# A decoder step on one core: neighbouring cache rows go to one partition, and keys are put in order when they are turned

## The reference, cut to what matters

```python
def gather_attention(q, k_all, v_all, idx, dist, table):
    kg, vg = k_all[:, safe], v_all[:, safe]
    logits = jnp.einsum('bthgd,btmhd->bhgtm', q, kg) * ATTN_SCALE + bias
    logits = jnp.where(valid, logits, NEG_INF)
    ...
    o = jnp.einsum('bhgtm,btmhd->bthgd', p, vg)

def dilated_sample(q, k_all, v_all, L, table):
    for w, r in ((128, 1), (512, 4), (2048, 16)):
        idx = L + t - r * jnp.arange(w // r + 1)[None, :]    # t = 0..7
        ...
    return combine_branches(outs, lses)
```

## Time and profile before

| | |
|---|---|
| median of 3 runs | 1210.07 us |
| profiled execution, its own time | 1210.34 us |
| its span | 1208.6 us |
| granted TensorE clock, mean | 0.937 |
| PE busy | 1070.4 us (89%) |
| DVE busy | 588.0 us (49%) |
| ACT busy | 470.0 us (39%) |
| POOL busy | 137.8 us (11%) |
| hardware DMA queue | 96764 packets, 179.89 MB |

### The profile page before, as it was taken

How to read it: one execution, slowest core, us unless ns; L and a number is a source line. 1 busy time by engine, 2 the same in 40 slices (tenths; PEclk the granted TensorE clock), 3 DMA queues, 4 the chain that set the end, 5 groups by cost and what they waited for, 6 DMA issues and landing times. The chain is left out here.

```text
span 1208.6 us, 16319 instructions
## 1 busy us (share of the span) xinstructions
PE 1070.4 (89%) x5923; PEld 869.0 (72%) x5924; DVE 588.0 (49%) x972; ACT 470.0 (39%) x736; POOL 137.8 (11%) x133
## 2 busy tenths in 40 slices
PE   5799999999699998878999539999999999999960
PEld 3699999998456566645888437877877778778740
DVE  5411113420056664334335466664599966649534
ACT  5311111001256653234213224554377655546324
POOL 0000000000100000000000011312234422224120
PEclk8699999999779999998999759999999999999985
DMA  6125111201560006886322563678699966789338
GB/s 219 63 52 203 49 53 53 70 14 66 153 159 1 2 1 176 266 228 189 145 105 79 189 247 94 208 273 278 215 382 391 377 209 204 271 293 395 110 70 312
DMA packets 104161, 207.34 MB, mean 172 GB/s; under 512 B 12648, under 2 KB 47249, under 8 KB 104075
## 3 DMA queue, kind: packets, MB, share of 16 engines
q1 hardware_dynamic: 96764, 179.89, 41.7%
q0 software_dynamic: 7344, 26.74, 9.1%
HBM read 175.75 MB, written 36.55 MB: 176 GB/s over the span
## 5 line engine op out<-in xcount | busy, mean ns | idle before, releaser
L540 PE MATMUL bank<-xT_hi,w_hi 128*128 128x384 f32 (+1 forms) x432 | 96.3, 331 | 5.4 <-DVE w_rest L403 5.4
L540 PE MATMUL bank<-xT_rest,w_hi 128*128 128x384 f32 (+1 forms) x432 | 96.0, 330 | 0.0
L540 PE MATMUL bank<-xT_hi,w_rest 128*128 128x384 f32 (+1 forms) x432 | 95.7, 329 | 0.0
L1853 POOL DMA_INDIRECT x_rows<-y_out,out_id x24 | 58.5, 2437 | 216.0 <-DVE rows L1908 199.1
L994 DVE CUSTOM_DVE_ANT_0 logit<-score,stage 128x256 f32<-128x256 f32 (+7 forms) x80 | 46.1, 614 | 75.9 <-DMA sink_pick<-in_sink_pick 55.5
L1737 DVE TENSOR_TENSOR down_rest<-w_down,down_hi 128x2048 fp32r<-128x2048 f32 x32 | 71.9, 2289 | 20.9 <-ACT down_hi L1732 20.0
L540 PEld LDWEIGHTS bank<-xT_hi,w_hi 128*128 128x128 f32 x432 | 74.5, 190 | 5.6 <-issue 5.6
L1961 PE MATMUL gate<-gate_hi,rowsT_hi 128*128 128x512 f32 x192 | 77.2, 402 | 0.7 <-ACT rowsT_hi L1867 0.7
L1962 PE MATMUL gate<-gate_rest,rowsT_hi 128*128 128x512 f32 x192 | 77.7, 404 | 0.0
L1995 PE MATMUL y<-down_hi,hidT_hi 128*128 128x512 f32 x192 | 76.9, 401 | 0.0
L1962 PE MATMUL up<-up_rest,rowsT_hi 128*128 128x512 f32 x192 | 75.6, 394 | 0.0
(11 more groups left out here) (277 smaller groups left out, 2034.2 us busy)
## 6 DMA issues: line engine op xcount, KB each, us to landing
w_gate<-in_w_gate SPq DMA_DIRECT2D x16, 2048.0 KB, 12.1
w_up<-in_w_up SPq DMA_DIRECT2D x16, 2048.0 KB, 12.3
w_down<-in_w_down SPq DMA_DIRECT2D x16, 2048.0 KB, 12.7
stage<-in_w_in SPq DMA_DIRECT2D x6, 1536.0 KB, 7.1
k_cache<-in_cache_b_k SPq DMA_DIRECT2D x8, 768.0 KB, 7.9
bias_scratch<-bias_one_row SPq DMA_DIRECT2D x1, 5800.0 KB
mixT<-in_x_prompt SPq DMA_DIRECT2D x8, 512.0 KB, 4.0
x<-in_x_prompt SPq DMA_DIRECT2D x8, 512.0 KB, 4.0
```

What stands on the lines that cost most here:

```text
L540: ins = nc.tensor.matmul(bank[3 * (n % 2) + i][:, 0:m], w_tiles(wt, n // CH)[:, k, cols], xt[:, k, c:c + m], start=(k == 0 and x == 0), st ...
L1853: nc.gpsimd.indirect_dma_start(out=io["x1"], out_offset=bass.IndirectOffsetOnAxis(ap=out_id[:, :], axis=0), in_=y_out[:, :], in_offset=Non ...
```

## The change

Two or four neighbouring cache rows go to one partition: of the far rows partition p holds two neighbours (4 pairs of each 8), of the near rows four. Block k of the buffers then holds every second row (k = 0, 1) or every fourth (k = 2 to 5). Each buffer's far part is one DMA instead of two. The keys return to their order when the transposed block is copied: `key_cols(k)` gives the columns of `kT_s` that a block goes to, with a step of 2 or 4. Scores, bias and softmax stay as they are. The transposes of the probabilities pick the same columns with the same step, so that their rows match the V buffers. The semaphore counts follow the number of DMAs.

```diff
-                out, src = kT_s[:, b % 2, :, P * k:P * k + P], src[:, 0:BW].rearrange("p (g c) -> p g c", c=P)
+                out, src = kT_s[:, b % 2, :, key_cols(k)], src[:, 0:BW].rearrange("p (g c) -> p g c", c=P)
...
+        def key_cols(k):
+
+            return slice(k, FARK, 2) if k < 2 else slice(FARK + k - 2, FARK + NEARK, 4)
...
-                for k in range(2):
-                    sp.dma_start(k_cache[:, b % 2, k, :], io["cache_b_k_far"][b][k]).then_inc(k_loaded[b % 2], 16)
+                sp.dma_start(k_cache[:, b % 2, 0:2, :], io["cache_b_k_far"][b]).then_inc(k_loaded[b % 2], 16)
...
-                for k in range(2):
-                    sp.dma_start(to[:, k, :], io["cache_b_v_far"][b][k]).then_inc(loaded, 16)
+                sp.dma_start(to[:, 0:2, :], io["cache_b_v_far"][b]).then_inc(loaded, 16)
...
-                    pe.wait_ge(k_loaded[b % 2], 48 * (r + 1))
+                    pe.wait_ge(k_loaded[b % 2], 32 * (r + 1))
...
-                        ins = nc.tensor.transpose(bank[0:m, P * (x - k):P * (x - k) + P], probs[:, r % 2, P * x:P * x + m], ident[:, :])
+                        cols = key_cols(x) if x < SKT else slice(FARK + NEARK, SK)
+                        ins = nc.tensor.transpose(bank[0:m, P * (x - k):P * (x - k) + P], probs[:, r % 2, cols], ident[:, :])
...
-                    pe.wait_ge(v_place(b)[1], 64 if r == PAIRS - 1 else 64 * (r + 1))
+                    pe.wait_ge(v_place(b)[1], 48 if r == PAIRS - 1 else 48 * (r + 1))
...
-        io[f"cache_b_{n}_far"] = [[rows[b, 256 * k:256 * k + 256].rearrange("(a r) c -> a r c", r=16)[:, 0:NT, :]
-                                   for k in range(2)] for b in range(NB)]
-        io[f"cache_b_{n}_near"] = [rows[b, SEQ // 2:SEQ].rearrange("(k p) c -> p k c", p=P) for b in range(NB)]
+        io[f"cache_b_{n}_far"] = [rows[b, 0:SEQ // 2].rearrange("(a r k) c -> a r k c", r=8, k=2)[:, 0:NT // 2, :, :] for b in range(NB)]
+        io[f"cache_b_{n}_near"] = [rows[b, SEQ // 2:SEQ].rearrange("(p k) c -> p k c", p=P) for b in range(NB)]
```

## The result

The changed kernel takes 1213.64 us, median of 10 runs (1212.23 to 1215.58), against 1209.62 us of the kernel before in the same series (1208.55 to 1210.62). The ratio is 1.0029, 95% interval 1.0016 to 1.0041: 2 to 5 us slower. The prediction was 1214.5 us with a range of 1209.2 to 1219.5. The profiled execution took 1212.32 us (span 1210.6), 2.0 us more than that of the kernel before; the median lies 1.3 us above it.

What follows compares the result with a forecast made beforehand. The prediction took PE's chain with copies in it as the bound. Key pieces 3.4 us plus transposes of the probabilities 1.0 made 4.4 us; 1210.34 + 4.4 - 0.27 gave 1214.5 us, range 1209.2 to 1219.5.

Steps and rivals of the forecast that it cites:

- What bounds the stage: Sample attention, about 461 to 552 us: a chain through PE with copies by ACT and DVE in it.
- The one visible wait for a load: Keys of sequence 7 in r = 3: 1.3 us wait goes, piece shrinks from 6.60 to 6.07, gaining 0.5 us.
- The price of a stepped copy: Copies into kT_s: 0.30 us more for each of all 48, with loads' gain counted in, 3.4 us.
- Transposes of the probabilities: 24 transposes with stepped stationary operand: 0.04 us more each, 1.0 us in all.
- The clock: PE's lower clock in parts of the stretch: about 1.7 us either way on every case, outside the sum.
- A: Stepped writes and loads cost nothing on ACT, DVE and PE: -0.5 us, 1209.6 us; chance 0.33 with clock scatter.
- B: Copies into kT_s: surcharge near the upper bound, 0.60 us each, giving 1220 to 1223 us; chance 0.16.
- D: Loads in longer runs move no faster, r = 3 keeps its wait: 1215.0 us, or 1210.1 in A; no chance given.
- C: PE's clock shifts: gain of 1.2 to 2.6 us, as easily a loss; gain below 1207.7 us has chance 0.05.

Runs made afterwards that it cites:

- loads_only: Changed kernel's long-run loads without steps, bias rows permuted once by GpSimd instead; ratio 0.9991 against the kernel before.
- again_after: The changed kernel as it is, measured once more; ratio 1.0023 against the kernel before.
- step_six_everywhere: Changed kernel with a step of six in all blocks, for copies and transposes of the probabilities; ratio 1.0072 against the kernel before.
- stepped_turns_only: Changed kernel with copies into kT_s back to runs, only the transposes of the probabilities stepped; ratio 0.9993 against the kernel before.
- step_two_everywhere: Changed kernel with pairs of neighbouring rows everywhere, so no step above two; ratio 1.0009 against the kernel before.
- price_by_step: Changed kernel with another column pattern per sequence's copies and weight-load steps 1, 2, 3, 6 by round; no total time or ratio given.

## Why the prediction was right, and where its terms were off

**What bounds the stage:** right. It is PE's chain with the copies in it. The one visible wait for a load was worth even less than the 0.5 us that I allowed it: loads_only keeps round 3 at 6.60 us, so this term failed: it was worth 0. It took round 2's length as the floor. But a round has its copies dealt out by the number of the group: in round 3 DVE has the first one, so that ACT's third copy and exp come later (exp starts 2.60 us into the piece, in round 2 2.28), and it is DVE again, behind its scaling, that has the first copy of the second sequence. 6.60 is that round's own floor.

**The price of a stepped copy:** 0.30 us, from GpSimd's rows of one element in four and in six, and it came out at 0.29 (DVE) and 0.37 (ACT). The step that failed is "I take 0.30 us, for all 48": 16 copies have a step of two, for which no row existed, and they pay nothing. GpSimd's two rows, for steps of six and four, agreed with each other, and for DVE and ACT too both steps lie on the dear side. So the keys came to 1.96 us (2.31 in again_after) and not 3.4; step_six_everywhere, where all 48 pay, comes to 4.1.

The Trainium skill, "Vector Engine (DVE) Microarchitecture Reference", section "Measured stream behaviour on trn2", asks for two adjacent words for full rate: the traces disagree at a step of two (0.56 us). Its lower figure for a destination that hops at every element, 1.71 against 1.054 ns, is near what DVE pays at four and six (0.28 and 0.30 us more for 384 elements, 0.7 to 0.8 ns each); its 2.50 ns is not seen here. The Trainium skill, "SBUF — State Buffer", note on cachelines, asks for two accesses to one 16-byte line, which fits every pattern of these runs, but goes on that four fp32 can be stepped for free, and they cannot: 0.29 us.

**Transposes of the probabilities:** 1.0 us predicted, 0.4 measured (0.37 in stepped_turns_only). The weight load did grow, from 140 to 208 ns, more than the 0.04 us that I took, but seven in a row take 1.10 us instead of 0.98 and the rest hides behind matmuls.

**The clock:** counted as a scatter of 1.7 us about the sum and not in it. The profiles of the changed kernel have 1.6 and 1.9 us of it, and step_six_everywhere 4.4. But loads_only and step_two_everywhere have 3.4 and 3.2 us in theirs without a ratio that is clear of 1. So the forecast lay within 1 us of the result partly by luck: terms that were 2.1 us too large met clock time that was not in the sum. What is shown: 2.3 us by the pieces, and 2 to 5 us by the runs. That longer gaps of PE bring more of the lower clock is suggested by step_six_everywhere, and by the scores of round 3, which take 5.47 to 5.75 us in all five profiles with longer copies of the near blocks only and exp in its old place. They take 4.13 in the kernel before, stepped_turns_only and price_by_step. But they take 5.83 in loads_only and step_two_everywhere, whose copies are not longer, so it isn't shown.

**Rivals.** A (no cost, 1209.6) and B (0.60 us a copy) are out by the copies' rows. D is out: the runs of 3072 and 6144 bytes move at 394 GB/s. C was a part of it, on the side that adds time.

## What to carry to other kernels

A wait for a DMA in the waits view is worth what remains after the next-latest releaser, so look, for that very instance, at what the other engines are still doing: here 1.26 us of waiting was worth 0 in PE's chain, and after one reordering of exp the same loads were worth 1.7 us, at other waits. A layout that gets longer runs in memory by stepping columns is paid on the engines; permute the small table (the bias) once instead of every key. And a price read at one step doesn't hold for a smaller one: in these runs two float32 elements in a row that share 16 bytes are written by DVE at full pace, and by ACT within 0.03 us. When a stretch of the profile is longer, look first whether the same matmuls took longer in it: of 3.07 us between two kernels, 1.70 were clock.

## What the runs showed of the hardware that was not expected

- Copies of 128x384 float32 from PSUM to SBUF take on DVE 0.56 us with runs, 0.56 with a step of two, 0.68 to 0.74 with three, 0.83 to 0.87 with four, 0.86 with six; on ACT 0.49, 0.52, 0.70, 0.86, 0.87.
- A weight load of 128 float32 columns takes PE 140 ns on average from a run, 206 with a step of two, 231 with six: unlike a copy, it pays at two.
- Loads from HBM in runs of 1536 bytes kept the DMA engines full at 289 GB/s; in runs of 3072 and 6144 bytes they moved 394.
- The granted clock alone made the same 91 us of work 3.4 us longer in one execution (loads_only) than in another (before): two groups of 24 score matmuls took 5.83 us and not 4.13.
